# Low parts of the first expert blocks placed between the routing steps of both token tiles, gates from product 44

## The chip, the cores and the metric

The kernel runs on one core of a Trainium2 chip. The metric is device time in microseconds (us); less is better. The core has TensorE (PE; matmuls, with weight loads shown apart as PEld), VectorE (DVE), ScalarE (ACT) and GpSimd (POOL), and SyncE (SP), whose queue issues nearly all transfers here.

## The reference

One decoder layer over 256 positions of width 1024: attention of three kinds, a projection and a layer norm give x1; then PEER, a retrieval over 128 x 128 = 16384 single-neuron experts; then another layer norm. The part around the change is PEER:

```
qh = (x1 @ w_query).reshape(T, 8, 256)
s1 = qh[..., :128] @ sub_keys_1.T ; s2 = qh[..., 128:] @ sub_keys_2.T
v1, i1 = top_k(s1, 16) ; v2, i2 = top_k(s2, 16)
cand = v1[:, None] + v2[None, :]          # 16 x 16 a head
top_s, top_j = top_k(cand, 16) ; experts = i1*128 + i2 at top_j
gate = softmax(top_s)
y = sum over the chosen experts of gate * gelu(x1 . u_expert) * v_expert
```

## The kernel before

The kernel doesn't gather experts. It multiplies x1 with all 16384 columns of `expert_u` in 128 **products** (`expert_in(c)`, one for each block of 128 experts, 256 tokens wide), applies GELU, multiplies by a dense gate matrix that is zero for experts not chosen, and multiplies with all of `expert_v` in 128 output products (`expert_out`).

For accuracy a block's f32 weights are split in two fp32r parts. ScalarE makes the high part (`u_split`, L948, a cast into one of `UH = 3` buffers `hi`), VectorE the low part (`fill`, L1319, raw minus high, written over the raw block). A product has 24 matmuls: for each of 8 slices of the width, high x high, high x low of x1, and low x high of x1. It waits for `u_lo`, its low part. `u_split(c)` waits for product c - 3, since it takes that one's `hi` buffer; in the loop over the products it stands behind `gelu(c - 3)` on ScalarE. Raw blocks have `UR = 6` buffers: `load_u(c)` on SP waits for product c - 6.

**Routing.** TensorE first makes the queries: 32 query products (`query(j)`, 16 for each of two tiles of 128 tokens, weights from a ring of 7 buffers loaded by `load_query(j)`, which waits for query j - 7), each followed by its subkey scores. ScalarE copies each query and each score out of PSUM (L960, L942). VectorE finds the top 16 of the scores in pairs of two score rows (`subkey_tops(t, b)`, eight pairs a tile, each two rounds of MAX8 L1325, FIND_INDEX8 L1328 and one MATCH_REPLACE8 L1334), then `route(t)`: candidates (L1359), top 16 of them, and for four groups of two heads three long steps that turn positions into expert numbers (`is_equal` L1373, multiply L1378, reduce L1382; called eq steps), then small steps L1386 to L1392. The softmax weights follow (L1410 to L1414), and `route_ready` lets TensorE turn the routes (`turn_routes`, L751, ahead of product `NTURN`).

**Gates.** From product `N0` on, a group of four tokens' gates is built ahead of each product (`gates(g)`, 64 groups, matmuls of one-hot rows made by VectorE, ScalarE and GpSimd) and multiplied into the arena. Blocks below `N0` have their GELU output in the arena by then; the arena columns of the others are filled with ones, by GpSimd memsets (L401 to L404, L418 to L420) and ScalarE copies, and each of those blocks is multiplied in later by VectorE (`block_gate`).

**Orders.** Each engine's order is written out by hand. VectorE before: tile 0's pairs, `topped`, `route(0)`, three low parts, then for tile 1 eight pairs with one low part behind each, `route(1)` with 16 low parts, the softmax weights, and low parts up to number 31. The raw blocks 2 and 3 lie where tile 0's scores are, so SP waits for `topped` before it loads them. GpSimd's first two memsets (L401, L402) wait for the last query's copy.

Of the kernel before, what the change touches and what calls it, by code (L numbers as in the profile page):

```python
# [33 lines left out]
TAKEN = -3e38  # L34
TWO_PI = (6.28125, 0.0019350051879882812, 2 * np.pi - 6.28125 - 0.0019350051879882812)
PI_IN = 3.1415925
N0 = 32
NROUTE = 27
NTURN = 28
POOL_HOT = 2  # L40
GN = S // 4
UR, UH = 6, 3
# [81 lines left out]
NU = len(UNITS)  # L124
EARLY = 6
FIRST1 = 8


def peer_layer_kernel(nc, x, xT, memT, positions, w_tok, w_memq, w_memk, w_memv, w1k, w1v, w2k, w2v, peT,
                      w_out, ln1, wq, subk, uT, pv, ln2, consts, out):  # L130
    with ExitStack() as ctx:
# [197 lines left out]
        @block.sync  # L329
        def _(sp):  # L330
            for k in range(0, KD, 2):
                sp.dma_start(xT_sb[:, k:k + 2, :], xT[:, k:k + 2, :]).then_inc(l_first[k // 2], 16)
                sp.dma_start(w_t[:, k:k + 2, 0:512], w_tok[:, k:k + 2, 0:512]).then_inc(l_first[k // 2], 16)
            for n, (c0, w) in list(enumerate(CHUNKS))[1:]:
                sp.dma_start(w_t[:, :, c0:c0 + w], w_tok[:, :, c0:c0 + w]).then_inc(l_w[n], 16)
            sp.dma_start(w_mq, w_memq).then_inc(l_wmq, 16)
            sp.dma_start(memT_sb, memT).then_inc(l_mT, 16)
            sp.dma_start(w_mk, w_memk).then_inc(l_wmk, 16)
            sp.dma_start(w_mv, w_memv).then_inc(l_wmv, 16)
            sp.dma_start(w1[:, 0], w1k).then_inc(l_w1, 16)  # L340
            sp.dma_start(w1[:, 1], w1v).then_inc(l_w1, 16)
            sp.dma_start(xs[:, :, :], x).then_inc(l_x, 16)
            sp.wait_ge(pe_proj, T * len(CHUNKS))
            sp.dma_start(w_o, w_out).then_inc(l_wo, 16)

            def load_query(j):
                if j >= RING:
                    sp.wait_ge(pe_q, j - RING + 1)
                sp.dma_start(ring[:, j % RING, :], wq[j % (2 * PH)]).then_inc(l_ring[j % RING], 16)

            def load_u(c):
                if c >= UR:
                    sp.wait_ge(pe_h, c - UR + 1)
                sp.dma_start(u_raw(c), uT[c]).then_inc(u_in[c % UR], 16)

            for j in range(RING):
                load_query(j)
            sp.wait_ge(pe_hid, 2)
            sp.dma_start(ln_sb, ln1.partition_broadcast(P)).then_inc(l_ln1, 16)
            for j in range(RING, 22):  # L360
                load_query(j)
            sp.wait_ge(pe_mix, 2)
            sp.wait_ge(x1_ready, 2)
            for c in (0, 1, 4, 5):
                load_u(c)
            for j in range(22, 4 * PH):
                load_query(j)
            sp.wait_ge(topped, 1)
            for c in (2, 3):
                load_u(c)  # L370
            for c in range(UR, NK):
                load_u(c)
            for c in range(NK):
                if c == 0:
                    sp.wait_ge(pe_g, GN)
                elif 4 <= c < VR:
                    sp.wait_ge(pe_h, NK)
                elif c >= VR:
                    sp.wait_ge(pe_y, c - VR + 1)
                sp.dma_start(raw[:, v_slot(c), :], pv[c]).then_inc(v_in[c % VR], 16)  # L380
            for t in range(T):
                for half in range(2):
                    cs = slice(half * 512, (half + 1) * 512)
                    sp.wait_ge(y_ready, 2 * t + half + 1)
                    sp.dma_start(out[t * P:(t + 1) * P, cs], xs[:, t, cs]).then_inc(stored, 16)
            sp.wait_ge(stored, 32 * T)
# [414 lines left out]
        def _(act):  # L801
# [142 lines left out]
            def u_split(c):  # L944
                act.wait_ge(u_in[c % UR], (c // UR + 1) * 16)
                if c >= UH:
                    act.wait_ge(pe_h, c - UH + 1)
                nc.scalar.copy(hi[:, c % UH, :], u_raw(c)).then_inc(u_hi, 1)  # L948

            for j in range(4 * PH):  # L950
                if j == 2:
                    root(1)
                if j == 4:
                    save_x1_turn(1)
                if 26 <= j < 26 + UH:
                    u_split(j - 26)
                act.wait_ge(pe_q, j + 1)
                if j >= 2:
                    act.wait_ge(pe_sk, j - 1)
                nc.scalar.copy(qT[:, j % 2, :], ps[:, 4 + j % 2, 0:P]).then_inc(q_saved, 1)  # L960
                if j >= 1:
                    save_scores(j - 1)
# [73 lines left out]
        def _(dve):  # L1036
# [3 lines left out]
            def did(ins):  # L1040
                count[0] += 1
                ins.then_inc(dve_chain, 1)

            def settle():
                dve.wait_ge(dve_chain, count[0])
# [269 lines left out]
            def fill(n=1):  # L1315
                for _ in range(n):
                    c = filled[0]
                    dve.wait_ge(u_hi, c + 1)
                    v.tensor_tensor(u_rest_of(c), u_raw(c), hi[:, c % UH, :].bitcast(F32), ALU.subtract).then_inc(u_lo, 1)  # L1319
                    filled[0] += 1  # L1320

            def top16(jobs, mixed):
                for o in (0, 8):
                    for vals, _, s in jobs:
                        did(v.max(vals[:, o:o + 8], s))  # L1325
                    settle()
                    for vals, idx, s in jobs:
                        did(v.max_index(idx[:, o:o + 8], vals[:, o:o + 8], s))  # L1328
                    if mixed:
                        fill()  # L1330
                    if o == 0:
                        settle()
                        for vals, _, s in jobs:
                            did(v.match_replace(s, vals[:, 0:8], s, TAKEN))  # L1334
                        if mixed:
                            fill()
                    settle()

            def subkey_tops(t, b):
                dve.wait_ge(sk_saved, 2 * PH * t + b + 2)  # L1340
                top16([(V[:, t, i, :], IX[:, t, i, :], sc[t][:, i, :]) for i in (b, b + 1)], False)

            def spread(mixed, n=1):
                if mixed:
                    fill(n)

            def route(t, mixed):
                did(v.tensor_copy(IF, IX[:, t, :, :]))
                settle()
                i1 = IF.rearrange("p (h a) k -> p h a k", a=2)[:, :, 0, :]  # L1350
# [5 lines left out]
                for r0, r, c in RUNS:  # L1356
                    sl = slice(OFF[r0], OFF[r0] + r * c)
                    for o, a1, a2 in ((cand, v1, v2), (cande, i1, i2)):
                        did(v.tensor_tensor(o[:, :, sl].rearrange("p h (r c) -> p h r c", r=r),  # L1359
                                            a1[:, :, r0:r0 + r].unsqueeze(3).to_broadcast([P, PH, r, c]),  # L1360
                                            a2[:, :, 0:c].unsqueeze(2).to_broadcast([P, PH, r, c]), ALU.add))
                spread(mixed)
                settle()
                top16([(tv[:, hh, :], ti[:, hh, :], cand[:, hh, :]) for hh in range(PH)], mixed)
                v.tensor_tensor(te[:, t], tv, tv[:, :, 0:1].to_broadcast([P, PH, TK]), ALU.subtract).then_inc(g_shift, 1)

                did(v.tensor_copy(tf, ti))
                settle()
                for h0 in range(0, PH, 2):
                    eqh = eq[:, h0 * TK * NCAND:(h0 + 2) * TK * NCAND].rearrange("p (h k c) -> p h k c", h=2, k=TK)  # L1370
                    eqm = eqh.rearrange("p h k c -> p (h k) c")
                    tfl = tf[:, h0:h0 + 2, :].rearrange("p h k -> p (h k)")
                    did(v.tensor_tensor(eqm, tfl.unsqueeze(2).to_broadcast([P, 2 * TK, NCAND]),  # L1373
                                        kc[:, K_IOTA:K_IOTA + NCAND].unsqueeze(1).to_broadcast([P, 2 * TK, NCAND]),
                                        ALU.is_equal))
                    spread(mixed)
                    settle()
                    did(v.tensor_tensor(eqh, eqh, cande[:, h0:h0 + 2, :].unsqueeze(2).to_broadcast([P, 2, TK, NCAND]),  # L1378
                                        ALU.mult))
                    spread(mixed)  # L1380
                    settle()
                    did(v.tensor_reduce(tfl, eqm, AX_X, ALU.add))  # L1382
                    spread(mixed)
                settle()
                tfl = tf.rearrange("p h k -> p (h k)")
                did(v.tensor_scalar(ex[:, t, 0, :], tfl, 1.0 / NK, -(NK - 1) / (2.0 * NK), ALU.mult, ALU.add))  # L1386
# [4 lines left out]
                settle()  # L1391
                did(v.scalar_tensor_tensor(out=ex[:, t, 1, :], in0=ex[:, t, 0, :], scalar=-float(NK), in1=tfl,  # L1392
                                           op0=ALU.mult, op1=ALU.add))
                settle()

            subkey_tops(0, 0)
            split_x1(1)
            for b in range(2, 2 * PH, 2):
                subkey_tops(0, b)
            settle()  # L1400
            v.tensor_scalar(lnst[:, 0, 6:7], lnst[:, 0, 7:8], 0.0, None, ALU.add).then_inc(topped, 1)
            route(0, False)
            fill(3)
            for b in range(0, 2 * PH, 2):
                subkey_tops(1, b)
                fill()
            route(1, True)
            for t in range(T):
                dve.wait_ge(g_exp, t + 1)
                did(v.tensor_reduce(gs[:, 0:PH], te[:, t], AX_X, ALU.add))  # L1410
# [152 lines left out]
```

## Time and profile before

| | |
|---|---|
| time, median of 3 runs | 1105.05 us (1103.86 to 1106.35) |
| the profiled execution: its own time | 1104.46 us |
| its span, first to last instruction | 1102.6 us |
| mean granted TensorE clock | 0.964 of 2.4 GHz |
| PE busy | 1045.7 us (95%) |
| DVE busy | 772.2 us (70%) |
| ACT busy | 433.0 us (39%) |
| POOL busy | 109.0 us (10%) |
| read from HBM | 174.33 MB, 159 GB/s over the span |

The products run from 303.8 us to about 740 us of the span, the output products from 743.4 to about 1091. In a row of a timeline a bracket gives the idle time of the engine in front of the instruction and what ended it. Times of matmuls overlap, since they are pipelined: what counts is from start to start. The same holds for short instructions of VectorE and ScalarE, whose recorded lengths overlap the next start a little.

### The profile page before, as it was taken

How to read it: one execution, taken by the hardware profiler on the slowest of the kernel's cores; microseconds unless marked ns; L12 is line 12 of the kernel's file. 1: busy time of each engine (PE TensorE's matmuls, PEld its weight loads, DVE VectorE, ACT ScalarE, POOL GpSimd, SP SyncE). 2: the span in 40 equal slices, each digit the busy share in tenths (PEclk: the TensorE clock that was granted, in tenths of full speed). 3: DMA queues.
4: the chain of work that ended last, by engine and by line, in shares of the span. 5: the costliest groups of instructions: out<-in, count | busy, mean ns of one | idle time of the engine just before them, and what ended most of it. 6: DMA issues, size and time to landing. Idle time of an engine off the chain costs nothing.

```text
span 1102.6 us, 17393 instructions
## 1 busy us (share of the span) xinstructions
PE 1045.7 (95%) x6508; PEld 912.4 (83%) x6508; DVE 772.2 (70%) x1817; ACT 433.0 (39%) x767; POOL 109.0 (10%) x210
## 2 busy tenths in 40 slices
PE   6999889899598999999999999989999999999996
PEld 2458766489588999999999999988888888888885
DVE  1253345368999969999999975556666666666667
ACT  0242233322333464554554544443333333333341
POOL 1000000000300043333333300000000000000000
PEclk9989659999899999999999999999999999999999
DMA  9607100059244554444444445546555555555551
GB/s 336 284 1 286 39 1 0 1 172 341 80 135 143 183 170 138 136 147 140 134 147 142 135 159 185 183 180 239 197 195 191 191 193 192 197 196 195 192 191 38
DMA packets 48610, 176.50 MB, mean 160 GB/s; under 512 B 5120, under 2 KB 6160, under 8 KB 47248
## 3 DMA queue, kind: packets, MB, share of 16 engines
q1 hardware_dynamic: 48128, 173.82, 45.9%
q0 software_dynamic: 400, 1.58, 0.4%
q8 instruction: 52, 0.85, 0.3%
q14 instruction: 30, 0.25, 0.1%
HBM read 174.33 MB, written 1.05 MB: 159 GB/s over the span
## 4 chain that ended last, share of the span: by engine, by line
PE 83%; DVE 14%; DMA 1%; ACT 1%; issue 1%; SPq 0%; DVEq 0%
PE ps L431 81%; DVE lo L1319 2%; DVE arena L1328 1%; DVE arena L1378 1%; DVE arena L1382 1%; DVE arena L1373 1%; DMA arena<-in_w_tok 1%; PE ps L579 1%; DVE arena L1325 1%; DVE arena L1334 1%; DVE hi L1319 0%; DVE ahl L1319 0%; DVE arena L1359 0%; ACT arena L874 0%; PE ps L490 0%
## 5 line engine op out<-in xcount | busy, mean ns | idle before, releaser
L431 PE MATMUL ps<-x1hl,hi 128*128 128x256 f32 x2216 | 380.3, 286 | 18.6 <-DVE lo L1319 17.2
L431 PEld LDWEIGHTS ps<-x1hl,hi 128*128 128x128 f32 x2216 | 328.1, 192 | 20.8 <-issue 12.2
L431 PE MATMUL ps<-hi,ahl 128*128 128x512 f32 x992 | 266.6, 390 | 3.0 <-DVE lo L1473 3.0
L431 PEld LDWEIGHTS ps<-hi,ahl 128*128 128x128 f32 x992 | 186.8, 188 | 42.0 <-issue 3.1
L1024 ACT CAST hi<-slab 128x1024 fp32r<-128x1024 f32 x128 | 134.5, 1053 | 206.9 <-PE ps L431 206.9
L431 PE MATMUL ps<-x1hl,lo 128*128 128x256 f32 x688 | 195.0, 283 | 0.0
L1473 DVE TENSOR_TENSOR lo<-slab,hi 128x1024 fp32r<-128x1024 f32 x128 | 155.9, 1218 | 0.0
L431 PE MATMUL ps<-lo,ahl 128*128 128x512 f32 x496 | 153.3, 390 | 0.0
L431 PEld LDWEIGHTS ps<-x1hl,lo 128*128 128x128 f32 x688 | 132.2, 192 | 0.0
L431 PE MATMUL ps<-arena 128*128 128x128 f32 (+5 forms) x800 | 114.4, 304 | 4.8 <-ACT arena L874 3.6
L431 PEld LDWEIGHTS ps<-arena 128*128 128x128 f32 (+2 forms) x800 | 101.8, 202 | 19.9 <-issue 9.5
L1319 DVE TENSOR_TENSOR lo<-slab,hi 128x1024 fp32r<-128x1024 f32 x86 | 106.0, 1234 | 16.9 <-ACT hi L948 16.6
L431 PE MATMUL ps<-arena,slab 128*128 128x512 f32 (+2 forms) x256 | 105.3, 565 | 10.7 <-DMA arena<-in_w_tok 9.7
L948 ACT CAST hi<-slab 128x1024 fp32r<-128x1024 f32 x107 | 111.2, 1040 | 0.4 <-DMA slab<-in_uT 0.4
L431 PEld LDWEIGHTS ps<-lo,ahl 128*128 128x128 f32 x496 | 93.6, 189 | 19.5
L1485 DVE CAST ahl<-arena 128x256 fp32r<-128x256 f32 x124 | 36.4, 294 | 103.6 <-PE ps L431 103.5
L973 ACT ACTIVATE gel<-ps 128x256 f32<-128x256 f32 x96 | 36.9, 384 | 163.8 <-PE ps L431 163.8
L431 PEld LDWEIGHTS ps<-arena,slab 128*128 128x128 f32 x256 | 48.9, 224 | 53.3 <-issue 39.1
L412 POOL TENSOR_SCALAR slab<-slab,n 128x128 f32<-128x128 f32 x128 | 78.0, 622 | 149.8 <-PE ps L431 149.6
L431 PE MATMUL ps<-slab 128*128 128x128 f32 (+1 forms) x576 | 84.1, 290 | 0.0
L431 PEld LDWEIGHTS ps<-slab 128*128 128x128 f32 x576 | 76.0, 194 | 2.9 <-issue 1.0
L1426 DVE TENSOR_SCALAR slab<-slab 128x128 f32<-128x128 f32 x256 | 75.9, 336 | 0.0
(193 smaller groups left out, 860.2 us busy)
## 6 DMA issues: line engine op xcount, KB each, us to landing
slab<-in_pv SPq DMA_DIRECT2D x128, 512.0 KB, 3.2
slab<-in_uT SPq DMA_DIRECT2D x107, 512.0 KB, 3.3
arena<-in_wq SPq DMA_DIRECT2D x32, 512.0 KB, 4.9
ahl_raw<-in_uT SPq DMA_DIRECT2D x21, 512.0 KB, 3.2
arena<-in_w_tok SPq DMA_DIRECT2D x2, 2048.0 KB, 16.3
arena<-in_w_out SPq DMA_DIRECT2D x1, 4096.0 KB, 12.1
arena<-in_w_tok SPq DMA_DIRECT2D x4, 512.0 KB, 8.1
arena<-in_w_tok SPq DMA_DIRECT2D x1, 1792.0 KB, 19.0
```

The lines of the kernel that those rows point to most:

```text
L412: ins = nc.gpsimd.tensor_scalar(hot(g)[:, 0, q, :], iota, n2[:, g % 2, q:q + 1], None, ALU.is_equal)
L431: return nc.tensor.matmul(o, lhsT, rhs, start=start, stop=stop, skip_group_check=True)
L579: last = nc.tensor.transpose(ps[:, 2, b * P:(b + 1) * P], xb[u % 3][:, b * P:(b + 1) * P], ident)
L948: nc.scalar.copy(hi[:, c % UH, :], u_raw(c)).then_inc(u_hi, 1)
L973: nc.scalar.activation(gel[:, c % 2, :], ps[:, c % 2, 0:S], ACT.Gelu).then_inc(gelu_done, 1)
L1024: nc.scalar.copy(hi[:, c % VH, :], raw[:, v_slot(c), :]).then_inc(v_hi, 1)
L1319: v.tensor_tensor(u_rest_of(c), u_raw(c), hi[:, c % UH, :].bitcast(F32), ALU.subtract).then_inc(u_lo, 1)
L1325: did(v.max(vals[:, o:o + 8], s))
L1328: did(v.max_index(idx[:, o:o + 8], vals[:, o:o + 8], s))
L1426: ins = v.tensor_scalar(hot(g)[:, 1, q, :], iota, slotT[:, 0, tok], slotT[:, 2, tok], ALU.is_equal, ALU.mult)
L1473: v.tensor_tensor(lo[:, v_slot(c), :], raw[:, v_slot(c), :], hi[:, c % VH, :].bitcast(F32), ALU.subtract).then_inc(v_lo, 1)
L1485: v.tensor_copy(o[:, 0, :], a).then_inc(a_hi, 1)
```

## The change

It changes VectorE's order: five low parts go into `route(0)` (one behind the reduce of the second and of the third group of heads, three in the fourth group), two instead of one into each pair of tile 1's subkey tops (the first behind the first FIND_INDEX8 round), and 18 instead of 16 into `route(1)`. So 39 low parts, not 27, stand before the routes are ready; `NROUTE`, `NTURN` and `N0` grow by 12, and the gates begin at product 44. On ScalarE the casts of blocks 0, 1 and 2 go from ahead of queries 26, 27 and 28 to ahead of queries 22, 23 and 26. On SP the wait for `topped` and the loads of blocks 2 and 3 go in front of query loads 28 to 31. The first memset covers `arena[:, N0 * S:A_S1]`, so 6144 columns instead of 9216.

```diff
-N0 = 32
-NROUTE = 27
-NTURN = 28
+N0 = 44
+NROUTE = 39
+NTURN = 40
...
+FIRST_HI = (22, 23, 26)
...
-            for j in range(22, 4 * PH):
+            for j in range(22, 28):
                 load_query(j)
             sp.wait_ge(topped, 1)
             for c in (2, 3):
                 load_u(c)
+            for j in range(28, 4 * PH):
+                load_query(j)
...
-                if 26 <= j < 26 + UH:
-                    u_split(j - 26)
+                if j in FIRST_HI:
+                    u_split(FIRST_HI.index(j))
...
-            def top16(jobs, mixed):
+            def top16(jobs, fills):
                 for o in (0, 8):
                     for vals, _, s in jobs:
                         did(v.max(vals[:, o:o + 8], s))
+                    if o and fills > 2:
+                        fill()
                     settle()
                     for vals, idx, s in jobs:
                         did(v.max_index(idx[:, o:o + 8], vals[:, o:o + 8], s))
-                    if mixed:
+                    if fills:
                         fill()
                     if o == 0:
                         settle()
                         for vals, _, s in jobs:
                             did(v.match_replace(s, vals[:, 0:8], s, TAKEN))
-                        if mixed:
+                        if fills > 2:
                             fill()
                     settle()
...
-                spread(mixed)
-                settle()
-                top16([(tv[:, hh, :], ti[:, hh, :], cand[:, hh, :]) for hh in range(PH)], mixed)
+                if t:
+                    fill()
+                settle()
+                top16([(tv[:, hh, :], ti[:, hh, :], cand[:, hh, :]) for hh in range(PH)], 4 * t)
...
                                         ALU.is_equal))
-                    spread(mixed)
+                    if t or h0 == 6:
+                        fill()
...
                                         ALU.mult))
-                    spread(mixed)
+                    if t or h0 == 6:
+                        fill()
                     settle()
                     did(v.tensor_reduce(tfl, eqm, AX_X, ALU.add))
-                    spread(mixed)
+                    if t or h0 >= 2:
+                        fill()
...
                                            op0=ALU.mult, op1=ALU.add))
-                settle()
-
-            subkey_tops(0, 0)
+                if t:
+                    fill()
+                settle()
+
+            subkey_tops(0, 0, 0)
...
-            route(0, False)
-            fill(3)
+            route(0)
             for b in range(0, 2 * PH, 2):
-                subkey_tops(1, b)
-                fill()
-            route(1, True)
+                subkey_tops(1, b, 2)
+            route(1)
```

## Rows read from the trace of the kernel before

**Rows 1.** Windows view, 291.5 to 396 us; columns: length, PE, PEld, DVE, ACT, POOL, clock, DMA.
```profile
291.50:396.00 104.50, 85.90 (x685) 83.71 (x685) 99.77 (x269) 41.22 (x62) 12.06 (x3) 0.95 0.41 137
```

**Rows 2.** Timeline of TensorE: start, us, engine, line, instruction, count, idle before.
```profile
303.81 0.77 PE L431 MATMUL ps<-x1hl,hi 128*128 128x256 f32 x2 [12.02 <-DVE lo L1319]
...
394.86 0.82 PE L751 MATMUL ps<-slab,arena 128*128 128x128 f32 x6
...
395.43 0.84 PE L431 MATMUL ps<-x1hl,hi 128*128 128x256 f32 x5
...
407.02 1.06 PE L431 MATMUL ps<-slab 128*128 128x128 f32 x8
...
410.79 1.06 PE L431 MATMUL ps<-slab 128*128 128x128 f32 x8
```

**Rows 3.** The chain that ended last, in order of time: start, us, what.
```profile
303.81 4.35 PE ps L431 x24
...
395.67 344.75 PE ps L431 x2912
```

**Rows 4.** Timeline of ScalarE, in the queries and in the products.
```profile
272.61 0.27 ACT L960 COPY gel<-ps 128x128 f32<-128x128 f32 x1 [1.52 <-PE ps L431]
...
283.52 1.05 ACT L948 CAST hi<-slab 128x1024 fp32r<-128x1024 f32 x1 [0.37 <-DMA slab<-in_uT]
...
648.29 0.38 ACT L973 ACTIVATE gel<-ps 128x256 f32<-128x256 f32 x1 [2.45 <-PE ps L431]
```

**Rows 5.** Timeline of VectorE: routing of tile 0.
```profile
264.22 0.15 DVE L1401 TENSOR_SCALAR lnst<-lnst 128x1 f32<-128x1 f32 x1
...
284.93 1.82 DVE L1373 TENSOR_TENSOR arena<-arena,slab 128x1600 f32<-128x1600 f32 x1
...
290.38 1.81 DVE L1373 TENSOR_TENSOR arena<-arena,slab 128x1600 f32<-128x1600 f32 x1
...
292.23 1.82 DVE L1378 TENSOR_TENSOR arena<-arena 128x1600 f32<-128x1600 f32 x1
...
295.94 2.94 DVE L1386 TENSOR_SCALAR arena<-arena 128x128 f32<-128x128 f32 x1
```

**Rows 6.** Timeline of GpSimd: its memsets.
```profile
291.02 7.78 POOL L401 MEMSET arena<- 128x9216 f32 x1 [286.30 <-ACT gel L960]
...
298.74 3.00 POOL L402 MEMSET arena<- 128x3392 f32 x1
...
402.22 3.26 POOL L420 MEMSET arena<- 128x3776 f32 x1
```

**Rows 7.** Timeline of VectorE: low parts (L1319) amid the routing of tile 1, and later.
```profile
330.35 1.22 DVE L1319 TENSOR_TENSOR lo<-slab,hi 128x1024 fp32r<-128x1024 f32 x1
...
331.49 0.48 DVE L1325 MAX8 arena<-arena 128x8 f32<-128x128 f32 x2
...
332.67 0.09 DVE L1334 MATCH_VALUE_LOAD arena<-arena 128x8 f32 x1
...
334.50 1.23 DVE L1319 TENSOR_TENSOR lo<-slab,hi 128x1024 fp32r<-128x1024 f32 x1
...
342.18 1.22 DVE L1319 TENSOR_TENSOR ahl<-ahl_raw,hi 128x1024 fp32r<-128x1024 f32 x1
...
345.79 1.21 DVE L1319 TENSOR_TENSOR lo<-slab,hi 128x1024 fp32r<-128x1024 f32 x1
...
387.96 0.23 DVE L1386 TENSOR_SCALAR arena<-arena 128x128 f32<-128x128 f32 x1
...
389.07 0.29 DVE L1410 TENSOR_REDUCE arena<-arena 128x8 f32<-128x128 f32 x1
...
390.60 1.22 DVE L1319 TENSOR_TENSOR lo<-slab,hi 128x1024 fp32r<-128x1024 f32 x1
...
403.97 1.23 DVE L1319 TENSOR_TENSOR lo<-slab,hi 128x1024 fp32r<-128x1024 f32 x1 [1.79 <-ACT hi L948]
```

**Rows 8.** Timeline of SyncE's queue, 200 to 420 us.
```profile
259.56 17.38 SPq L349 DMA_DIRECT2D arena<-in_wq  x10
```

More of the change, by code:

```diff
@@ L1334, in top16, with subkey_tops, route @@
                             did(v.match_replace(s, vals[:, 0:8], s, TAKEN))
-                        if mixed:
+                        if fills > 2:
                             fill()
                     settle()
-            def subkey_tops(t, b):
+            def subkey_tops(t, b, fills):
                 dve.wait_ge(sk_saved, 2 * PH * t + b + 2)
[L1341 to L1347, printed above, removed]
+                top16([(V[:, t, i, :], IX[:, t, i, :], sc[t][:, i, :]) for i in (b, b + 1)], fills)
+            def route(t):
                 did(v.tensor_copy(IF, IX[:, t, :, :]))
@@ L1393, in route @@
                                            op0=ALU.mult, op1=ALU.add))
+                if t:
+                    fill()
                 settle()
-            subkey_tops(0, 0)
+            subkey_tops(0, 0, 0)
             split_x1(1)
             for b in range(2, 2 * PH, 2):
-                subkey_tops(0, b)
+                subkey_tops(0, b, 0)
             settle()
             v.tensor_scalar(lnst[:, 0, 6:7], lnst[:, 0, 7:8], 0.0, None, ALU.add).then_inc(topped, 1)
-            route(0, False)
-            fill(3)
+            route(0)
             for b in range(0, 2 * PH, 2):
-                subkey_tops(1, b)
-                fill()
-            route(1, True)
+                subkey_tops(1, b, 2)
+            route(1)
             for t in range(T):
```

## The prediction

> **What bounds the kernel now.** I read the chain that ended last first. It is TensorE almost throughout, with one foreign stretch, the routing on VectorE between the last query and the steady products. From 395.67 us the chain is TensorE for 344.75 us without a break [rows 3]. I then took the windows of the stretch ahead of that: in the 104.5 us from 291.5 to 396 TensorE is busy 85.9 and idle 18.6, at a mean granted clock of 0.95, while VectorE is busy 99.77 [rows 1]. TensorE's timeline shows where: 12.02 us between the last subkey product and product 0 (start 303.81), ended by L1319, the subtraction that makes a block's low part; the other 6.6 us are shorter waits and gaps between products [rows 1, 2].
>
> A product with a gate group takes 410.79 - 407.02 = 3.77 us [rows 2]. From the start of product 28 at 395.43 [rows 2] to the end of the unbroken piece, 395.67 + 344.75 = 740.42 [rows 3], lie 100 products, 64 of them with a group: 344.99 - 64 x 3.77 = 103.7 for the other 36, 2.88 each. A group so costs 0.89. Behind 395 nothing but TensorE's own work counts; what can be won lies in front of it.
>
> **The time of an unbroken run.** TensorE's queries end at 303.81 - 12.02 = 291.79 [rows 2]. From there to gate group 0 the kernel before does 32 products and the turn of the routes (394.86 to 395.43, 0.57, plus 0.07 by which the four products behind it exceed 4 x 2.88; I take 0.64 [rows 2]): 32 x 2.88 + 0.64 = 92.8 us of work in 407.02 - 291.79 = 115.23. The excess is 22.4 us: 18.6 of idle; about 1.2 because product 0 took 4.35 us [rows 3], at a clock not yet back at its upper level of 2.4 GHz after the idle stretch; and some 2.6 of restarts and small gaps.
>
> **Part 1: five low parts inside the routing of tile 0.** Needed is low part c at 291.79 + 2.88c. The first stands behind the second group's reduce, where VectorE was at 284.93 [rows 5]. One low part holds VectorE 331.49 - 330.35 = 1.14 us [rows 7]. A group of three eq steps takes 290.38 - 284.93 = 5.45, a step 1.85 [rows 5]. Starts of the five: 284.9; 284.93 + 1.14 + 5.45 = 291.5; + 1.14 + 1.85 = 294.5; 297.5; 300.5. Part 0 is ready at 286.1, long before TensorE asks, so product 0 starts at 291.8. Parts 1 to 4 are ready at 292.7, 295.6, 298.6, 301.6, against 294.7, 297.6, 300.4, 303.3. Parts 3 and 4 also need a high part that ScalarE makes only behind products 0 and 1. Its GELU and cast take 0.38 and 1.05 [rows 4], so they come 1.4 us behind a product's end: 296.1 and 299.0, before VectorE gets there. The idle 12.02 goes, and with it the slow clock of product 0.
>
> **Part 2: the stall at 295.94 goes as well.** The small TENSOR_SCALAR at L1386 took 2.94 us [rows 5] and takes 0.23 in tile 1 [rows 7]. Its end, 298.88, is that of GpSimd's first memset, 291.02 + 7.78, and the next one, in the way of L1388, runs from there to 298.74 + 3.00 [rows 6]. Now the first memset fills 6144 columns and not 9216, so by its row it takes 5.2 us: both end at 299.2. VectorE reaches L1386 at 295.94 + 5 x 1.14 = 301.6, behind them. Four small steps later (389.07 - 387.96 = 1.1 [rows 7]) tile 0 is routed at 302.8, as late as before, but with five low parts made.
> The memsets now lie beside low parts 1 and 2 and the eq steps. L1378 at 292.23 took 1.82 beside the first memset, and a low part at 403.97 took 1.23 beside a memset of 402.22 to 405.48 [rows 5 to 7], so I count nothing. The Trainium skill (SBUF — State Buffer, Who interferes with whom) says that VectorE and GpSimd share a port pair as an exclusive lock, taken by copy, cast and tensor_scalar in a two-port mode, while a tensor_tensor meets only GpSimd instructions that read; both rows agree. Were every VectorE instruction locked out, it would be the second rival below.
>
> **Part 3: two low parts in each pair of subkey tops.** A pair with one took 334.50 - 330.35 = 4.15 us, so with two 5.29, or 2.65 per product against TensorE's 2.88. This is the tightest place. The new low part stands 332.67 - 331.49 = 1.18 behind a pair's start, the other 1.83 behind the new one's end [rows 7]. From 302.8: part 5 ready at 305.1 (needed 306.2), part 6 at 308.1 (309.1), parts 7 and 8 at 310.4 and 313.4 (311.9 and 314.8). The margin is 1.0, then grows by 0.46 a pair until the high parts hold VectorE: part c can begin only 1.4 us behind product c-3, which leaves a margin of 5.76 - 1.4 - 1.22 = 3.1. Before, this section ran at 4.15 a product: here most of the shorter waits go.
>
> **Part 4: eighteen in the routing of tile 1.** The longest steps between two low parts' starts were 345.79 - 342.18 = 3.61 and one like it [rows 7], each eating 0.7 of the margin; an eq step with its low part takes about 1.73 + 1.14 = 2.87, which keeps it. The margin stays above 1.6. The chain to the gates' weights is 390.60 - 389.07 = 1.5 us [rows 7]; low part 38 is ready by about 400 and the weights by about 402, while TensorE turns the routes ahead of product 40, at 291.8 + 115.2 = 407.0. So TensorE doesn't wait there.
>
> **Part 5: blocks 2 and 3 sooner, queries 28 to 31 behind them on SP.** The wait on `topped` is met at 264.4 [rows 5]. SP's ten query loads of before went out over 259.56 to 276.9, one a query [rows 8], so number 27 goes at about 268.6; the wait costs nothing, and blocks 2 and 3 follow at once. Before, block 2 was asked for at 277 and landed at 283.5 [rows 4, 8], 6.5 us; now that gives 275.4, and its cast at query 26 comes at about 279. The casts at queries 22 and 23 (1.05 us each) fit ScalarE's idle 1.52 in front of every query's copy [rows 4]. Query load 28 is asked for a query behind TensorE's 21st, some 12 us before its use; 1 MB ahead of it costs those 6.5 at most.
>
> **Part 6: the gates 12 products later.** 64 groups and 128 products stay; 12 VectorE gatings of blocks go, under TensorE's steady work, worth nothing. The step from the products to the output products stays as it is.
>
> **Sum.** 1104.46 (the profiled execution's own time, 0.6 below the median of the three runs) - 22.4 = 1082.1 us, with 0.1 for the first product's start: **1082.2**. More than 22.4 can't be won, since TensorE then has no gap between 291.8 and the end of the products; below that lies only the scatter of runs (1103.86 to 1106.35), 2 us.
>
> **Rivals.**
> 1. VectorE late in the pairs. Parts 5 to 8 have 1.0 us; if the added low part breaks the pairing of steps and a pair costs 6.2, not 5.29, TensorE waits 0.44 a pair and restarts 16 times at 0.1: 3.5 + 1.6 = 5.1, 1087.3. It begins at 5.76 a pair. Against it: a pair's 4.15 is 3.01 of work plus 1.14. Chance 0.12.
> 2. The memsets lock out the low parts. Part 1 would wait from 291.5 to 296.2 and be ready at 297.4, 2.7 late, with parts 4 to 6 then about 1.3 later still: 4 us, 1086.2. Rows 6 and 7 speak against it. 0.04.
> 3. The wait moves: the routes are ready 22 us late and TensorE stands at product 40. VectorE's work from 264.4 (at most 402) would have to reach 429; nothing shows it. 1104.5, chance 0.03.
> 4. Slower: `topped` holds up SP with query loads 28 to 31 behind it. It is met at 264.4 and delays a load only from 268.6 on, TensorE only from about 276 (needed 282.7, landing 6.5). To eat 22.4 us it must come after 298; a stray 3 us more gives 1107. Against: tile 0's tops hang on queries 0 to 15 alone. 0.05.
>
> **How the numbers follow.** My forecast, 1080 to 1084, has 0.76. The range reaches up over rivals 1 and 2, 1080.0 to 1087.5. A change within 0.2% (2.2 us) can't be told from none here: faster 0.92, same 0.03, slower 0.05.
>
> **What would show it.** TensorE's first product right behind the last subkey product, with no idle of 12 us, and a clock of 1.00 there; no waits for L1319 before the gates; L1386 at 0.23 in both tiles; gate group 0 at about 291.8 + 44 x 2.88 + 0.6 = 419.1, the last product ending near 718; the first cast of high parts near 271. I am wrong if waits for L1319 reappear in the pairs, if a low part beside the memset takes several us, or if query 28 waits for its ring.

## The result and the profile after

The changed kernel takes 1080.78 us (median of 4 runs, 1078.89 to 1081.23) against 1104.71 (4 runs, 1103.86 to 1106.35): ratio 0.9776, 95% interval 0.9756 to 0.9795. A second comparison of the same two kernels, against 15 runs of before, gave 0.9791 (0.9771 to 0.9810). The change makes the kernel 2.1 to 2.2% faster.

The forecast was 1082.2 with a range from 1080.0. The first ratio times the median of before is 0.9776 x 1104.71 = 1080.0 and to two decimals 1079.96, just under the range, while the median itself, 1080.78, is inside it; the second ratio gives 1082.2 of 1105.28. So the order of the low parts did what was forecast. What has to be explained is that the first ratio lies some 2 us below the forecast, where the prediction allowed for nothing but a scatter of 2 us.

The chain that ended last, after (start, us, what; compare [rows 3]):

```profile
291.94 115.66 PE ps L434 x962
407.60 0.66 PE ps L754 x6
408.25 310.19 PE ps L434 x2624
...
718.46 0.39 ACT gel L976
...
718.88 0.44 DVE arena L1455
...
719.72 0.43 DVE ahl L1492
720.15 1.15 DVE lo L1478
...
721.38 343.04 PE ps L434 x1512
```

VectorE's routing has left the chain. TensorE runs from the last subkey product to the turn of the routes and on to the last product, 718.42, without a break. TensorE's timeline has the ends of the pieces (compare [rows 2]):

```profile
291.94 0.46 PE L434 MATMUL ps<-slab,gel 128*128 128x128 f32 x2 [0.45 <-ACT arena L945]
...
407.43 0.82 PE L754 MATMUL ps<-slab,arena 128*128 128x128 f32 x6
...
419.60 1.06 PE L434 MATMUL ps<-slab 128*128 128x128 f32 x8
...
721.38 0.70 PE L434 MATMUL ps<-hi,ahl 128*128 128x512 f32 x2 [2.96 <-DVE lo L1478]
```

The queries end at 291.94 + 0.46 = 292.40, gate group 0 stands at 419.60 (forecast 419.1), the products end at 721.38 - 2.96 = 718.42. From the queries' end to the products' end it is 426.02 us; before it was 740.41 - 291.79 = 448.62 [rows 2]. That is 22.6 less where 22.4 was forecast. In the windows view the stretch up to the turn has no idle, at a clock of 1.00, where [rows 1] had 18.6 us of idle at 0.95:

```profile
292.40:408.25 115.85, 115.85 (x968) 115.85 (x968) 106.90 (x280) 56.66 (x86) 9.16 (x3) 1.00 0.53 178
```

VectorE after (compare [rows 5, 7]; L1322 is the low part, L1391 the old L1386):

```profile
285.54 1.22 DVE L1322 TENSOR_TENSOR lo<-slab,hi 128x1024 fp32r<-128x1024 f32 x1
...
292.12 1.22 DVE L1322 TENSOR_TENSOR lo<-slab,hi 128x1024 fp32r<-128x1024 f32 x1
...
294.99 1.22 DVE L1322 TENSOR_TENSOR lo<-slab,hi 128x1024 fp32r<-128x1024 f32 x1
...
297.86 1.22 DVE L1322 TENSOR_TENSOR lo<-slab,hi 128x1024 fp32r<-128x1024 f32 x1
...
300.72 1.22 DVE L1322 TENSOR_TENSOR hi<-slab,hi 128x1024 fp32r<-128x1024 f32 x1
301.85 0.22 DVE L1391 TENSOR_SCALAR arena<-arena 128x128 f32<-128x128 f32 x1
...
304.02 1.21 DVE L1322 TENSOR_TENSOR ahl<-ahl_raw,hi 128x1024 fp32r<-128x1024 f32 x1
...
306.85 1.21 DVE L1322 TENSOR_TENSOR lo<-slab,hi 128x1024 fp32r<-128x1024 f32 x1
...
309.02 1.21 DVE L1322 TENSOR_TENSOR lo<-slab,hi 128x1024 fp32r<-128x1024 f32 x1
...
311.85 1.21 DVE L1322 TENSOR_TENSOR lo<-slab,hi 128x1024 fp32r<-128x1024 f32 x1
...
319.70 1.22 DVE L1322 TENSOR_TENSOR ahl<-ahl_raw,hi 128x1024 fp32r<-128x1024 f32 x1 [0.58 <-ACT hi L951]
```

The five low parts begin at 285.5, 292.1, 295.0, 297.9 and 300.7 (forecast 284.9 to 300.5, for queries that end 0.6 sooner). The small step behind them takes 0.22 and not 2.94. In the pairs the steps from one low part's start to the next are 2.83 and 2.17, 5.0 for two low parts; at 319.70 VectorE begins to wait for ScalarE's high part, so from there it is held back by what TensorE has used up. GpSimd's memsets end at 299.73, ahead of the small step, and low parts 1, 2 and 3 ran beside them in 1.22 us each (compare [rows 6]):

```profile
291.63 5.23 POOL L404 MEMSET arena<- 128x6144 f32 x1 [286.92 <-ACT gel L963]
296.80 2.93 POOL L405 MEMSET arena<- 128x3392 f32 x1
```

What the change doesn't explain comes behind the products. The output products take 343.04 us in this execution and took 344.61 in the profiled one of before. The windows view of their first 23 us, before and then after, has the granted clock ahead of the last two numbers (DMA share, GB/s):

```profile
743.37:766.37 23.00, 23.00 (x95) 18.89 (x96) 14.64 (x24) 8.61 (x9) 0.62 (x1) 0.93 0.63 226
```

```profile
721.38:744.38 23.00, 23.00 (x101) 19.04 (x102) 15.54 (x27) 9.49 (x10) 0.62 (x1) 1.00 0.70 250
```

TensorE is idle 2.96 us ahead of them in both. Before, the clock dropped for part of the stretch behind that idle (0.93 in the mean); in this execution of the changed kernel it didn't.

### The profile page after: what moved, and what is told of

Same layout as the page of the kernel before. It is cut to its first block, busy times and chain, and to the rows that moved or that the text cites. A ratio compares the mean times of both kernels' runs of the same rounds, so it can differ in the third digit from the quotient of the medians.

```text
span 1079.0 us, 17356 instructions
## 1 busy us (share of the span) xinstructions
PE 1040.5 (96%) x6508; PEld 909.5 (84%) x6508; DVE 760.0 (70%) x1805; ACT 432.9 (40%) x767; POOL 105.8 (10%) x210
## 4 chain that ended last, share of the span: by engine, by line
PE 94%; DVE 2%; DMA 1%; ACT 1%; SPq 0%; issue 0%; DVEq 0%
PE ps L434 92%; DMA arena<-in_w_tok 1%; PE ps L582 1%; PE ps L493 0%; ACT arena L877 0%; PE ps L620 0%; DVE xs L1519 0%; DVE slab L1134 0%; SPq L333 0%; DVE xs L1513 0%; DVE arena L1507 0%; DVE arena L1216 0%; DVE xs L1504 0%; PE ps L644 0%; SPq L334 0%
## 5 line engine op out<-in xcount | busy, mean ns | idle before, releaser
L1322 DVE TENSOR_TENSOR lo<-slab,hi 128x1024 fp32r<-128x1024 f32 x86 | 106.0, 1233 | 14.4 <-ACT hi L951 14.4
L434 PE MATMUL ps<-arena,slab 128*128 128x512 f32 (+2 forms) x256 | 105.5, 566 | 11.1 <-DMA arena<-in_w_tok 10.3
L976 ACT ACTIVATE gel<-ps 128x256 f32<-128x256 f32 x84 | 32.2, 383 | 145.4 <-PE ps L434 145.4
```

The source lines that it names most:

```text
L434: return nc.tensor.matmul(o, lhsT, rhs, start=start, stop=stop, skip_group_check=True)
L976: nc.scalar.activation(gel[:, c % 2, :], ps[:, c % 2, 0:S], ACT.Gelu).then_inc(gelu_done, 1)
```

## The experiments

Most of what follows is read from three stretches of each profile: up to the end of the queries, from there to the end of the products, and from there to the end of the span (the idle of 2.96 us, the output products and the last norm). Each begins and ends with a row of TensorE's timeline, as above. In us:

| profile of | queries end | products' stretch | the rest | span |
|---|---|---|---|---|
| before | 291.79 | 448.62 | 362.2 | 1102.6 |
| before, second profile | 292.37 | 448.65 | 362.2 | 1103.2 |
| after | 292.40 | 426.02 | 360.6 | 1079.0 |
| after, second profile | 288.88 | 426.02 | 361.9 | 1076.8 |
| after, third profile | 292.91 | 426.03 | 363.3 | 1082.2 |
| after, fourth profile | 290.58 | 426.02 | 363.3 | 1079.9 |
| old_loads | 291.95 | 426.03 | 360.5 | 1078.5 |
| late_memset | 292.15 | 444.09 | 362.2 | 1098.4 |
| only_route0 | 289.40 | 437.00 | 363.4 | 1089.8 |
| only_pairs | 291.39 | 437.40 | 363.3 | 1092.1 |
| long_gap | 292.38 | 426.03 | 364.1 | 1082.5 |
| no_gap | 292.25 | 425.93 | 357.8 | 1076.0 |
| no_gap, second profile | 289.61 | 425.93 | 357.9 | 1073.4 |

The middle stretch repeats to 0.03 us. The other two don't. Their code is the same in before and after, but for the loads and casts in the last 28 us of the queries; that stretch takes 27.57 us in every profile (see below).

**The two kernels again.** Nothing is edited.

> The changed kernel once more, unchanged. Theory A: the step between the products and the output products is an idle of 2.96 us in both kernels, and the granted clock drops behind it in some executions and not in others, costing about 1.6 us; then this one may show either, and its time against the kernel before is 22.5 to 25 us less. Theory B: the clock is kept at that step because of the change; then this profile shows it kept again, as every other variant with the products' end moved does.

> The kernel before as a kernel of its own. Theory A: its clock behind the 2.96-us step is kept in some executions, so this profile may show no drop, and then the span is about 1101.0 and not 1102.6. Theory B: the drop belongs to this kernel: seen again, span 1102.6.

Measured: 1080.56 us (5 runs), ratio 0.9791 (0.9771 to 0.9810); the kernel before as a kernel of its own 0.9994 (0.9982 to 1.0007). This execution of the changed kernel did drop its clock, and ended its queries 3.5 us sooner than the first. Two more:

> The changed kernel, a third look. If the drop comes and goes with the way that an execution falls, this shows one of the two cases again: output products 343.0 us with the clock kept, or about 344.5 with the drop; and the first product starts between 288 and 292.5 us by how the clock fell in the attention stage, with the stretch from it to the last product at 426.0 us in every case.

> The changed kernel, a fourth look, for the same question: kept (343.0 us) or dropped (344.5), the products' stretch at 426.0 us.

They took 1084.09 and 1081.76 us. Over all eleven runs of the changed kernel the mean is 1081.3, over fifty runs of before 1104.6: 23.3 less, give or take 1.2 us (95%), against the 22.6 of the middle stretch. The first 23 us of the output products in the second and the third profile:

```profile
717.86:740.86 23.00, 23.00 (x95) 18.93 (x96) 14.65 (x24) 8.61 (x9) 0.61 (x1) 0.94 0.67 230
```

```profile
721.90:744.90 23.00, 23.00 (x90) 18.75 (x91) 13.70 (x24) 8.44 (x9) 0.62 (x1) 0.87 0.60 209
```

The same idle of 2.96 us is followed by a mean clock of 1.00, 0.94 or 0.87, and by a rest of 360.6, 361.9 or 363.3 us. Of ten profiled executions with this idle, eight dropped their clock (all three of before and late_memset, three of four of after, only_route0, only_pairs) and two kept it (after, old_loads). Theory B, that the change keeps the clock, fell with the second profile.

The head of the kernel scatters too: the queries of the changed kernel end between 288.88 and 292.91. The windows view of 60 to 120 us in the second and then the third profile, in the attention part, far ahead of the change:

```profile
60.00:120.00 60.00, 60.00 (x306) 45.46 (x305) 22.09 (x90) 20.73 (x61) 0.00 (x0) 0.93 0.37 149
```

```profile
60.00:120.00 60.00, 60.00 (x290) 44.91 (x289) 21.44 (x93) 18.12 (x52) 0.00 (x0) 0.87 0.35 140
```

TensorE is at work throughout in both, at a clock of 0.93 and of 0.87; the execution with the higher clock gets 306 matmuls done and the other 290. The scatter is complete when tile 0's tops are found (the instruction that lets `topped` go, here in the second and the third profile):

```profile
261.31 0.15 DVE L1408 TENSOR_SCALAR lnst<-lnst 128x1 f32<-128x1 f32 x1
```

```profile
265.34 0.15 DVE L1408 TENSOR_SCALAR lnst<-lnst 128x1 f32<-128x1 f32 x1
```

From it to the queries' end it is 288.88 - 261.31 = 27.57 and 292.91 - 265.34 = 27.57 us; before it was 291.79 - 264.22 = 27.57 [rows 5], and it is 27.56 to 27.58 in every other profile here. The moved loads and casts come behind it, so neither they nor the rest of the change move the queries' end.

**old_loads.** Changed kernel, loads and first casts as before:

```diff
-FIRST_HI = (22, 23, 26)
+FIRST_HI = (26, 27, 28)
...
-            for j in range(22, 28):
+            for j in range(22, 4 * PH):
                 load_query(j)
             sp.wait_ge(topped, 1)
             for c in (2, 3):
                 load_u(c)
-            for j in range(28, 4 * PH):
-                load_query(j)
```

> The changed kernel with the old order of loads and first casts (blocks 2 and 3 behind query load 31, casts ahead of queries 26, 27, 28). My theory: the moves of loads and casts are worth next to nothing alone. The cast of block 0 comes at about 279.6 and low part 0 is due on VectorE at 285; block 2 lands at about 283.5, its low part is due at 294.5. Time as that of the changed kernel, within 1 us (ratio to before 0.976 to 0.979). Rival: low parts 0 to 2 wait for the high parts and the products start late: 3 us or more slower than the changed kernel.

Measured: 1080.57 us (4 runs), ratio 0.9788 (0.9765 to 0.9812); products' stretch 426.03. The moves of loads and casts are worth nothing measurable.

**late_memset.** Kernel before, GpSimd's first memsets later:

```diff
             pool.wait_ge(x1_split, 4)
+            pool.wait_ge(u_lo, 1)
```

> The kernel before with one wait more: GpSimd's first memsets wait for low part 0. Theory of the lock: L1386 and L1388 take 0.23 us each instead of 2.94 and 2.90, low part 0 comes 5.4 us sooner, TensorE's idle is 6.6 us instead of 12.02: time 5.4 us less (ratio 0.995), and nothing is lost where the memsets now lie, beside subkey tops and low parts, which keep their 0.48 and 1.22 us. Rival, a lock for every instruction of VectorE: tops and low parts wait for the memsets (10.8 us), and the time stays or grows.

Measured: 1099.42 us, ratio 0.9937 (0.9914 to 0.9960), so 4.4 to 9.5 us less; the forecast was 5.4. VectorE, GpSimd and TensorE in this kernel (its L1387 is the L1386 of before, L1320 the low part, L1326 the MAX8 of the tops):

```profile
296.30 0.23 DVE L1387 TENSOR_SCALAR arena<-arena 128x128 f32<-128x128 f32 x1
296.56 0.23 DVE L1389 TENSOR_SCALAR arena<-arena 128x128 f32<-128x128 f32 x1
...
305.46 1.22 DVE L1320 TENSOR_TENSOR lo<-slab,hi 128x1024 fp32r<-128x1024 f32 x1 [1.66 <-ACT hi L949]
306.60 0.48 DVE L1326 MAX8 arena<-arena 128x8 f32<-128x128 f32 x2
```

```profile
298.78 7.80 POOL L402 MEMSET arena<- 128x9216 f32 x1 [294.06 <-DVE lo L1320]
306.51 2.94 POOL L403 MEMSET arena<- 128x3392 f32 x1
```

```profile
298.78 0.77 PE L432 MATMUL ps<-x1hl,hi 128*128 128x256 f32 x2 [6.63 <-DVE lo L1320]
```

The two small steps take 0.23 us once the memset is out of their way, and TensorE's idle falls from 12.02 to 6.63, 5.39 less. The low part at 305.46 and the MAX8 at 306.60, beside the memsets, keep their 1.22 and 0.48 us. Only 4.5 of the 5.4 us arrive: the stretch is 444.09 for 448.62. The rest goes at product 0, which took 4.35 us before [rows 3] and takes 5.23 here:

```profile
298.78 5.23 PE ps L432 x24
```

The clock came back later behind its start. The windows view of the first 4.5 us from it, in the kernel before and in this one, at a mean clock of 0.69 and of 0.50:

```profile
303.81:308.31 4.50, 4.50 (x27) 4.50 (x28) 4.36 (x16) 0.13 (x1) 0.00 (x0) 0.69 0.00 0
```

```profile
298.78:303.28 4.50, 4.50 (x21) 4.50 (x22) 4.36 (x16) 0.00 (x0) 4.50 (x1) 0.50 0.00 0
```

**only_route0.** Changed kernel, one low part behind each pair of tile 1 (31 ahead of the routes):

```diff
-N0 = 44
-NROUTE = 39
-NTURN = 40
+N0 = 36
+NROUTE = 31
+NTURN = 32
...
-                subkey_tops(1, b, 2)
+                subkey_tops(1, b, 0)
+                fill()
```

> The changed kernel, but with one low part behind each pair of tile 1's subkey tops, as before, instead of two in it (31 low parts ahead of the routes, gates from product 36). My theory: the idle before product 0 stays gone; the pairs pace TensorE at 4.15 us a product. Low part 5 comes at about 307, just as needed, low part 12 at 336.1 where an unbroken run needs it at 327: 9.1 us lost there, 1.5 in the routing of tile 1, and restarts: 11 us slower than the changed kernel, about 1092 (ratio 0.988). Rival, the pace of the pairs hardly matters because TensorE waits elsewhere: within 3 us of the changed kernel.

Measured: 1092.33 us, ratio 0.9894 (0.9875 to 0.9914); the stretch is 437.00, 11.0 over the changed kernel. TensorE's timeline in the pairs (two rows of nine waits):

```profile
308.40 0.50 PE L434 MATMUL ps<-x1hl,hi 128*128 128x256 f32 x2 [1.02 <-DVE lo L1322]
...
312.55 0.50 PE L434 MATMUL ps<-x1hl,hi 128*128 128x256 f32 x2 [1.02 <-DVE lo L1322]
```

A wait of 1.02 in every 4.15 us, no idle before product 0. The nine waits are 8.0 us of the 11.0. A product behind one takes 4.15 - 1.02 = 3.13 us beside the wait, 0.25 more than the 2.88 of an unbroken run; what is left was not followed up.

**only_pairs.** Changed kernel, no low part in the routing of tile 0 (37 ahead of the routes):

```diff
-N0 = 44
-NROUTE = 39
-NTURN = 40
+N0 = 42
+NROUTE = 37
+NTURN = 38
...
-                    if t or h0 == 6:
+                    if t:
                         fill()
...
-                    if t or h0 >= 2:
+                    if t:
                         fill()
...
             route(0)
+            fill(3)
```

> The changed kernel, but with no low parts inside the routing of tile 0 and three behind it, as before (37 ahead of the routes, gates from product 42). My theory: TensorE stands idle about 9.8 us before product 0 (12.02 less what the smaller memset gives back), starts it at the lower clock, and has no wait after that: 9.8 + 1.3 = 11.1 us slower than the changed kernel, about 1092 (ratio 0.988). Rival: with two low parts in a pair and TensorE late anyway, more waits of 1 us appear in the pairs and it is 14 us or more slower.

Measured: 1093.63 us, ratio 0.9901 (0.9882 to 0.9920); the stretch is 437.40, 11.4 over the changed kernel. This is the only wait of TensorE for a low part in it:

```profile
301.28 0.77 PE L434 MATMUL ps<-x1hl,hi 128*128 128x256 f32 x2 [9.89 <-DVE lo L1322]
```

Taken out one at a time, the pairs cost 11.0 us and the routing of tile 0 11.4, in sum 22.4 of the 22.6 that both together bring.

**long_gap and no_gap.** The first puts two more VectorE instructions into the idle behind the products:

```diff
                     dve.wait_ge(pe_h, NK)
+                    for _ in range(2):
+                        did(v.tensor_tensor(gel[:, :, :], gel[:, :, :], gel[:, :, :], ALU.mult))
+                        settle()
```

> The changed kernel with two VectorE instructions of 512 columns more (about 1.2 us together, on values no longer used) ahead of the first split behind the products, so the idle of 2.96 us there is about 4.2. Theory A (whether the clock drops at this step hangs on how the idle falls, and a longer idle drops it more surely): the granted clock drops in this profile and the time is 1.2 + 1.5 = 2.7 us over a changed kernel that kept it. Theory B (the clock is kept in the changed kernel whatever the idle): only 1.2 us over, no drop.

Measured: 1084.25 us, ratio 0.9820 (0.9799 to 0.9841). The idle is 4.41 us, the clock dropped, and the rest is 364.1: 3.5 over the changed kernel that kept its clock (1.45 of idle and about 2.0 of slower output products), 0.8 over the two profiles of the changed kernel that lost most to the clock (2.7 us). That is as theory A had it, but since a 2.96-us idle nearly always drops the clock too, this run tells little more.

The second takes the idle away. Its core (all reads of the high buffers turn by one as well):

```diff
-                    act.wait_ge(pe_h, NK)
+                    act.wait_ge(pe_h, NK if c else NK - 3)
...
-                nc.scalar.copy(hi[:, c % VH, :], raw[:, v_slot(c), :]).then_inc(v_hi, 1)
+                nc.scalar.copy(hi[:, (c + 3) % VH, :], raw[:, v_slot(c), :]).then_inc(v_hi, 1)
...
+                if c == NK - 2:
+                    v_split(0)
...
-                block_gate(c, GN)
+                if c < NK - 1:
+                    block_gate(c, GN)
...
                 if c == 0:
                     dve.wait_ge(pre_gated, GN)
+                    dve.wait_ge(pe_h, NK - 2)
+                if c == 1:
                     dve.wait_ge(gated, NK - N0)
                     dve.wait_ge(pe_h, NK)
...
                 a_split(c)
                 v_rest(c)
+                if c == 0:
+                    block_gate(NK - 1, GN)
```

> The changed kernel without the idle behind the products: block 0 of the second weights takes the high buffer that is free sooner (3 instead of 0, all others turned by one), its cast stands behind the GELU of product 126, and VectorE splits block 0's activations and makes low part 0 ahead of the last block's gating. TensorE goes from product 127 straight to output product 0, waiting at most 0.3 us. Theory A: 2.7 to 2.9 us less than the changed kernel, and 1.4 more against its executions with the drop: 1077.5 to 1078.5 (ratio 0.976). Rival: the wait only moves to output product 1 and more than half of the gain is lost.

> The version without the idle once more, on the chip on which the kernel before with the same edit runs. Its ratio should be 0.974 to 0.976 again, so the order of low parts is worth 22 us with the edit too: 22.4 less the scatter of the attention stage, and no part of it from the drop.

Measured: 1076.32 us, ratio 0.9746 (0.9728 to 0.9764), and again 1077.32 us, ratio 0.9756 (0.9739 to 0.9773). Its chain and TensorE at the step from products to output products:

```profile
291.79 115.66 PE ps L434 x962
...
408.10 653.34 PE ps L434 x4136
```

```profile
718.00 0.28 PE L434 MATMUL ps<-x1hl,lo 128*128 128x256 f32 x1
718.18 0.70 PE L434 MATMUL ps<-hi,ahl 128*128 128x512 f32 x2
```

No idle and no drop; the rest is 357.8 and 357.9 us, 2.8 less than after at its best and 5.5 less than at its worst. It is the fastest version here.

**before_no_gap.** The same edit on the kernel before.

> The kernel before with the edit of no_gap alone (no idle between the products and the output products). If the clock drop behind that idle belongs to the kernel before (seen in 3 profiles of 3, against 1 of 3 with the changed order of low parts and the same idle), the edit is worth 2.9 + 1.5 = 4.4 us here: ratio 0.996. If it belongs to neither and comes and goes, some 3 to 4.4 us: ratio 0.996 to 0.9975. The profile shows no idle and no drop there either way.

Measured: 1100.38 us (7 runs), ratio 0.9959 (0.9945 to 0.9974), 4.3 us by the medians. Idle and drop behind the products are gone here too (one piece of the chain, 687.89 us, from the turn on). Its span less its queries' end (295.32) is 807.0 where before has 810.8, 3.8 less, although its product 0 took 4.94 us and not 4.35. Without that it would be 4.4. So the step costs both kernels about the same, some 2.8 us of idle and 1.6 of slow clock.

## Why the prediction was right, and where it was wrong

**The unbroken run.** Right: 22.4 us of excess by its sum, 22.6 by the profile. The 0.2 lie within the rounding of its terms (2.88 taken 32 times).

**Part 1, low parts in the routing of tile 0.** Right within 0.4 us at each of the five, once the queries' end is taken off: the first two are exact, and each step with a low part behind it then takes 2.87 us where 2.99 was summed. Shown by itself in only_pairs: without them an idle of 9.89 us (forecast 9.8) and 11.4 us in all (11.1).

**Part 2, the memset's stall.** Right, and shown twice: the step is 0.22 long in the profile after, and late_memset takes 5.39 us from the idle of the kernel before. The rule of the Trainium skill that was set beside it (SBUF — State Buffer, Who interferes with whom) agrees with these rows: tensor_scalar waited, tensor_tensor kept its 1.22 beside a memset. MAX8 kept its 0.48 there too. Rival 2 is out.

**Part 3, the pairs.** Right in effect, pessimistic in size: a pair with two low parts takes 5.0 us, not 5.29. The sum added the low part's 1.14 to the pair as it was. But in before the low part stood behind the wait for the last FIND_INDEX8's result, and now it stands in front of such waits. The row ahead of a low part's start at 334.50 [rows 7], and the one ahead of the low part at 304.02 of the profile after:

```profile
334.18 0.29 DVE L1328 FIND_INDEX8 arena<-arena 128x8 uint32<-128x128 f32 x1
```

```profile
303.82 0.28 DVE L1333 FIND_INDEX8 arena<-arena 128x8 uint32<-128x128 f32 x1
```

It is 0.32 us from start to start in the first and 0.20 in the second, 0.12 saved at each of the two low parts, most of the 0.29. The same 0.12 is what part 1's steps are short of their sum. Low part 5 was ready at about 305.2, 1.6 ahead of its need at 292.40 + 14.4. Rival 1 is out: no wait of TensorE for a low part is left.

**Parts 4 and 6.** Right: gate group 0 at 419.60, the turn of the routes without a wait, nothing given back while the gates are built later. Rival 3 is out.

**Part 5, loads and casts.** Right: the first cast of a high part starts at 271.59 (forecast near 271) and block 2's at 279.63 (279), the moves cost nothing, and old_loads shows that they bring nothing either. `topped` holds up no query, since the 27.57 us from it to the queries' end are those of before: rival 4 is out.

**The step that failed** is the end of the sum: "More than 22.4 can't be won, since TensorE then has no gap between 291.8 and the end of the products; below that lies only the scatter of runs (1103.86 to 1106.35), 2 us." It took every part of the profiled execution outside the middle stretch as fixed. Two weren't. The output products of that execution contained a clock drop (344.61 us, where 343.04 is the time at the upper level), and the profiled execution of after had none: its span is 22.6 + 1.6 - 0.6 (queries that ended later) = 23.6 us shorter. And the queries' end moves from 288.9 to 292.9 between executions of one kernel. Three runs of before, within 2.5 us of each other, don't show that; over four profiles of the changed kernel the span goes from 1076.8 to 1082.2 with a middle stretch that never moves. With four runs on either side such a scatter is 2 us of ratio (0.9756 to 0.9795), and the lower edge should have been near 1078, not 1080.0: the lowest of the eleven runs is 1078.72. For the two profiled executions the cause of 1.6 us is shown (clock kept in one and dropped in the other). The other runs behind the first ratio have no profile, so how its 2 us divide between the clock drop and the queries' end is not shown. That the second ratio falls on 1082.2 to the decimal is luck, with an interval of 2 us on either side. Why this idle of 2.96 us sometimes keeps the clock, and why the attention part falls one way or the other, stays open.

## What to carry to other kernels

Work out what the bounding engine does without a gap, from the point where it could start to the point behind which it never waits, and place the filler work of the other engine so that each piece has a due time: both halves of this change were worth what that sum said, 11 us each, and the loads moved for their sake were worth nothing. Look in a profile for short instructions that end exactly with a memset of GpSimd; moving the memset gave 4.5 us alone by the profile. And before you set the lower edge of a range, split the span into the part that the change touches and the parts that it doesn't: an idle of 3 us in the untouched part can be worth up to 5.5 us with its clock drop, and does not repeat from run to run.

## What the runs showed of the hardware

After an idle of 2.96 us on TensorE the granted clock fell in eight of ten executions and stayed in two, with the same instructions around it: mean clocks of 0.93 or 0.94, of 0.87, or of 1.00 over the next 23 us, and 0, 1.3 to 1.6, or 2.7 us lost. It need not fall during the idle: in late_memset TensorE was at work again from 739.20, the clock was 1.00 up to 740.20 and 0.50 from 741.20 to 743.20. After 4.41 us of idle it fell in the one execution profiled. The forecast had counted a clock loss only for the 12-us idle. What product 0 loses behind a longer idle isn't set by the length of the idle alone either: behind 12.02 us it took 4.35, 4.39 and 4.94 us in three executions, and behind 6.63 us 5.23.
